# A mixture-of-experts kernel: expert choice in short pieces, scaled identities on ScalarE, late tiles summed on TensorE

## The reference, cut to what matters

```python
q = (xb @ w_q).reshape(PEER_BLOCK, PEER_HEADS, 2, PEER_DHALF)
s = jnp.einsum('nhpd,hpkd->nhpk', q, keys)            # 128 keys in each half
top_s, top_i = lax.top_k(s, 16)
cand = top_s[:, :, 0, :, None] + top_s[:, :, 1, None, :]
cand_idx = top_i[:, :, 0, :, None] * 128 + top_i[:, :, 1, None, :]
best_s, best_j = lax.top_k(cand.reshape(..., 256), 16)
idx = jnp.take_along_axis(cand_idx, best_j, axis=-1)
gsm = jax.nn.softmax(best_s, axis=-1)
act = jax.nn.gelu(jnp.einsum('nd,nhkd->nhk', xb, expert_u[idx]))
out = jnp.einsum('nhk,nhkd->nd', gsm * act, expert_v[idx])
```

## Time and profile before

| | before |
|---|---|
| median of three runs | 2196.28 us |
| the profiled execution | 2195.12 us |
| its span | 2193.3 us, granted PE clock 0.904 |
| busy: PE, DVE, POOL, ACT | 1674.3, 1528.5, 702.3, 466.5 us |
| fetches of expert rows | 576, 604.02 MB, 70.2% of the 16 DMA engines' span |
| weights and the rest | 123.92 MB, 17.4% |

### The profile page before, as it was taken

The page is one execution under the profiler, slowest core; times in us unless marked ns, Lnnn a source line. Parts: engine busy times, 40 slices in busy tenths (PEclk is TensorE's granted clock), DMA queues, the critical chain, the costliest instruction groups (busy, mean ns, idle before and its releaser), DMA issues.

```text
span 2193.3 us, 16524 instructions
## 1 busy us (share of the span) xinstructions
PE 1674.3 (76%) x5012; PEld 877.3 (40%) x5012; DVE 1528.5 (70%) x3429; ACT 466.5 (21%) x1250; POOL 702.3 (32%) x581
## 2 busy tenths in 40 slices
PE   8999977799978999979596556566655667666665
PEld 3699964344434455545252222222222222222221
DVE  2351248999977656658857888868787767767666
ACT  1061023222266420132211111112011111111111
POOL 0000013233322333223333343343433444445442
PEclk9999988999989999989798887788788899998898
DMA  8766578899878899969888998999898999999996
GB/s 276 251 200 218 195 246 319 329 340 352 309 275 290 313 363 378 351 245 377 330 323 331 356 348 344 359 369 381 327 354 336 374 412 403 420 413 413 404 408 282
DMA packets 203475, 730.08 MB, mean 333 GB/s; under 512 B 12957, under 2 KB 125991, under 8 KB 129521
## 3 DMA queue, kind: packets, MB, share of 16 engines
q0 software_dynamic: 82944, 604.02, 70.2%
q1 hardware_dynamic: 119190, 123.92, 17.4%
q10 hardware_dynamic: 1252, 1.09, 0.2%
HBM read 725.92 MB, written 3.06 MB: 332 GB/s over the span
## 4 chain that ended last, share of the span: by engine, by line
PE 37%; DMA 24%; DVE 23%; issue 10%; ACT 3%; POOL 2%; DVEq 0%; SPq 0%; ACTq 0%; POOLq 0%
DMA t_uv_rows<-in_expert_uv,t_arena 22%; PE bank L563 19%; PE v_sum L645 13%; PE bank L519 4%; DVE t_acc L1253 3%; DVE t_uv_rows L1237 3%; DMA t_uv_rows<-in_expert_uv,t_idx 2%; POOL t_uv_rows L484 2%; DVE t_diag L1261 1%; DVE t_arena L1210 1%; DVE t_arena L1211 1%; DVE t_arena L1212 1%; DVE t_arena L1155 1%; DVE t_arena L1156 1%; DVE t_arena L1159 1%
## 5 line engine op out<-in xcount | busy, mean ns | idle before, releaser
L645 PE MATMUL v_sum<-t_uv_rows,t_diag 128*128 128x512 f32 (+1 forms) x1536 | 855.1, 696 | 468.6 <-DVE t_diag L1261 468.4
L645 PEld LDWEIGHTS v_sum<-t_uv_rows,t_diag 128*128 128x128 f32 (+1 forms) x1536 | 307.0, 214 | 962.7 <-DVE t_diag L1261 661.7
L484 POOL DMA_INDIRECT t_uv_rows<-in_expert_uv,t_arena x384 | 464.5, 1210 | 634.2 <-PE v_sum L645 516.5
L1237 DVE CUSTOM_DVE_ANT_0 t_uv_rows<-t_uv_rows,t_arena 128x1024 f32<-128x1024 f32 x384 | 470.1, 1224 | 263.6 <-DMA t_uv_rows<-in_expert_uv,t_arena 259.1
L563 PE MATMUL bank<-t_arena,t_weights 128*128 128x192 f32 (+1 forms) x2560 | 642.2, 410 | 1.3 <-issue 0.9
L563 PEld LDWEIGHTS bank<-t_arena,t_weights 128*128 128x128 f32 x2560 | 453.4, 192 | 196.7 <-issue 47.3
L484 POOL DMA_INDIRECT t_uv_rows<-in_expert_uv,t_idx x192 | 237.4, 1236 | 831.9 <-PE v_sum L645 417.9
L821 ACT ACTIVATE t_gelus<-t_dots 128x1 f32<-128x1 f32 x576 | 115.4, 202 | 1402.8 <-DVE t_dots L1237 1402.6
L1237 DVE CUSTOM_DVE_ANT_0 t_uv_rows<-t_uv_rows,t_tok 128x1024 f32<-128x1024 f32 x192 | 234.9, 1224 | 99.7 <-DMA t_uv_rows<-in_expert_uv,t_idx 97.1
L1253 DVE SCALAR_TENSOR_TENSOR t_acc<-t_uv_rows,t_wts,t_acc 128x1024 f32<-128x1024 f32 x187 | 239.6, 1281 | 1.7 <-ACT t_wts L826 1.7
L1261 DVE TENSOR_SCALAR t_diag<-t_ident,t_gelus,t_arena 128x128 f32<-128x128 f32 x288 | 99.0, 344 | 3.6 <-ACT t_gelus L821 3.6
(11 more groups left out here) (162 smaller groups left out, 966.5 us busy)
## 6 DMA issues: line engine op xcount, KB each, us to landing
t_weights<-in_w_in SPq DMA_DIRECT2D x40, 1024.0 KB, 5.9
t_weights<-in_w_ada SPq DMA_DIRECT2D x24, 1024.0 KB, 5.6
t_weights<-in_w_q SPq DMA_DIRECT2D x16, 1024.0 KB, 5.6
t_weights<-in_w_branch_a SPq DMA_DIRECT2D x8, 1024.0 KB, 7.0
t_weights<-in_w_branch_b SPq DMA_DIRECT2D x8, 1024.0 KB, 5.3
t_weights<-in_w_out SPq DMA_DIRECT2D x8, 1024.0 KB, 6.8
t_uv_rows<-in_expert_uv,t_arena POOLq DMA_INDIRECT x384, 8.6
t_weights<-in_keys_t SPq DMA_DIRECT2D x20, 256.0 KB, 7.3
```

Of the source, the lines that this page charges most:

```text
L484: pool.indirect_dma_start(out=uv_rows[:, slot % NUV, :], out_offset=None, in_=A["expert_uv"], in_offset=bass.IndirectOffsetOnAxis(ap=idx_o ...
L645: ins = nc.tensor.matmul(v_sum[0:m, half], scaled, v_row(slot)[:, half], start=opens, stop=False)
L1237: V.tensor_tensor_reduce(out=row, in0=row, in1=h2_rows(t), scale=1.0, scalar=0.0, op0=ALU.mult, op1=ALU.add, accum_out=dots[:, k:k + 1]).t ...
```

## The change

The three parts of a choice unit become eleven: one for each of four key halves ("keytop", "key"), the sums ("sums"), one "best" for each of two heads, "parts", "match", "number" and "gates". Within key and best, instructions of different heads no longer run as a batch; each is linked to the one before. The pieces are dealt over more places: units of tiles 0 and 1 over places 1 to 31, those from (2, 2) to (4, 3) over the 160 places from `dense + 5` (before: over 51 places and then 40 places from `dense + 64`). The second eight queries of group 1 come one in each place from `dense`.

`on_vector` now takes slots 2, 5, 8, ... of tile 0 (21 of 64), four of five in tile 1 (102 of 128), and none in tiles 2 to 4. The scaled identity is built by ACT, behind the weight, with a scale column; it has six buffers. PE sums the two rows of a pair at the next place's beginning, ahead of that place's products, which is where the "sum" entry had them, but for one slot later. In tiles 2 to 4 the last row closes the sum, without a fold.

```diff
-NW, NUV, NDIAG, NBANK = 3, 6, 4, 6
+NW, NUV, NDIAG, NBANK = 3, 6, 6, 6
...
-    return [("keytop", t, y), ("pairtop", t, y), ("number", t, y)]
+    return ([("keytop", t, y)] + [("key", t, 4 * y + h) for h in (1, 2, 3)] + [("sums", t, y), ("best", t, 2 * y), ("best", t, 2 * y + 1)]
+            + [(k, t, y) for k in ("parts", "match", "number", "gates")])
...
+    start += [[u] for u in queries[:5] + first[:4] + [queries[5]] + first[4:7] + [queries[6]] + first[7:] + [queries[7]]]
...
+    deal(queries[8:] + [("tok", 1, 0), square, norm, ("ada", 0, 22), ("ada", 0, 23)], places, 0, PAIRS)
+    deal(choice_units(0, 1), places, 1, 5)
+    later = [u for t, y in ((0, 2), (0, 3), (1, 0), (1, 1), (1, 2), (1, 3)) for u in choice_units(t, y)]
+    deal(later, places, 5, CHOICE_PLACES)
...
+    deal(choice_units(2, 1), places, DENSE_PLACES + 1, dense + 4)
...
+        places[dense + n].append(unit)
+    deal([u for t, y in [(2, 2), (2, 3)] + [(t, y) for t in (3, 4) for y in range(4)] for u in choice_units(t, y)], places,
+         dense + 5, dense + 165)
...
+    first, dense = (TOPK * sum(TILE_STEPS[t] for t in tiles) for tiles in ((0,), group_tiles(0)))
+    return slot % 3 == 2 if slot < first else slot < dense and slot % 5 != 0
...
+            def sum_row(t, slot):
+
+                if on_vector(slot):
+                    return
...
+                opens = slot == min(n for n in tile_slots(t) if not on_vector(n))
+                closes = t > 1 and slot == tile_slots(t)[-1]
+                if opens and t:
+                    pe.wait_ge(v_read, t)
+                pe.wait_ge(diag_done, NTH_ROW[slot])
+                scaled = diag[:, (NTH_ROW[slot] - 1) % NDIAG, 0:m]
+                for half in (slice(0, 512), slice(512, D)):
+                    ins = nc.tensor.matmul(v_sum[0:m, half], scaled, v_row(slot)[:, half], start=opens, stop=closes)
+                ins.then_inc(v_tile if closes else pe_rows, 1)
+                if closes:
+                    pe.wait_ge(v_tile, t + 1)
+                    pe.sem_inc(pe_rows, 1)
...
+                for slot in tile_slots(t)[-2:]:
+                    sum_row(t, slot)
+                if t > 1:
+                    return
...
+                elif role == "pair":
+                    here = slot_of(g, b[0], 2 * b[1])
+                    for slot in (here - 2, here - 1):
+                        if slot in tile_slots(g):
+                            sum_row(g, slot)
...
+                    nc.scalar.activation(gelus[:, k:k + 1], dots[:, k:k + 1], ACT.Gelu_apprx_tanh).then_inc(gelu_done, 1)
+                    act.wait_ge(gelu_done, slot + 1)
+                    nc.scalar.activation(wts[:, k:k + 1], gelus[:, k:k + 1], ACT.Copy,
+                                         scale=gsm_of(t)[:, at:at + 1]).then_inc(weight_done, 1)
+                    if not on_vector(slot):
+                        nth_row = NTH_ROW[slot]
+                        if nth_row > NDIAG:
+                            act.wait_ge(pe_rows, nth_row - NDIAG)
+                        act.wait_ge(weight_done, slot + 1)
+                        m = NS if t == 0 else P
+                        unit = ident2[:, :] if t == 0 else ident[:, :]
+                        nc.scalar.activation(diag[:, (nth_row - 1) % NDIAG, 0:m], unit, ACT.Copy,
+                                             scale=wts[:, k:k + 1]).then_inc(diag_done, 1)
...
+            def key_top(t, h):
...
+                link(V.max(top_v[:, 0:8], s))
+                link(V.max_index(top_i[:, 0:8], top_v[:, 0:8], s))
+                link(V.match_replace(less, top_v[:, 0:8], s, LOWEST))
+                if j == 3:
+                    dve.sem_inc(taken["score"], 1)
+                link(V.max(top_v[:, 8:16], less))
+                link(V.max_index(top_i[:, 8:16], top_v[:, 8:16], less))
...
+            def pair_top(t, h):
...
+                link(V.max(v[:, 0:8], c))
+                link(V.max_index(j[:, 0:8], v[:, 0:8], c))
+                link(V.match_replace(less, v[:, 0:8], c, LOWEST))
+                link(V.max(v[:, 8:16], less))
+                link(V.max_index(j[:, 8:16], v[:, 8:16], less))
...
+            def value(t, slot):
+                if not on_vector(slot):
+                    return
...
-                    if nth_row > NDIAG:
-                        dve.wait_ge(pe_rows, nth_row - NDIAG)
-                    m = NS if t == 0 else P
-                    unit = ident2[:, :] if t == 0 else ident[:, :]
-                    at = i * TOPK + k
-                    V.tensor_scalar(diag[:, (nth_row - 1) % NDIAG, 0:m], unit, gelus[:, k:k + 1], gsm_of(t)[:, at:at + 1],
-                                    ALU.mult, ALU.mult).then_inc(diag_done, 1)
...
-                before, own = values_at(t, i, j)
+                here = slot_of(t, i, 2 * j)
                 dot(t, i, 2 * j)
-                for step, k in before:
-                    value(t, step, k)
+                if here > tile_slots(t)[0]:
+                    value(t, here - 1)
                 dot(t, i, 2 * j + 1)
-                for step, k in own:
-                    value(t, step, k)
+                value(t, here)
+                if here + 1 == tile_slots(t)[-1]:
+                    value(t, here + 1)
```

More of the change, by code:

```diff
@@ L166, in schedule @@
     queries = query_units(0)
-    (key, pair, number), (key1, pair1, number1), (key2, pair2, number2) = (choice_units(0, y) for y in range(3))
+    first = choice_units(0, 0)
     square, norm, *copied = first_units(1)
-    start += [[u] for u in queries[:5] + [key, queries[5], pair] + queries[6:8] + [number]]
+    start += [[u] for u in queries[:5] + first[:4] + [queries[5]] + first[4:7] + [queries[6]] + first[7:] + [queries[7]]]
     s = staggered(start, lambda n, after: [])
@@ L194, in pair_entries @@
         if after:
-            close = j == PAIRS - 1 and i == TILE_STEPS[t] - 1
-            return [("sum", "pair", t, (i, j))] + [("both", "final", t, 0)] * close
+            return [("both", "final", t, 0)] * (j == PAIRS - 1 and i == TILE_STEPS[t] - 1)
         return [("pair", "pair", t, (i, j))] + [("both", "final", t - 1, j + 1)] * (t > 0 and i == 0 and j < 3)
@@ L629, in rows_of @@
                 return NS if t == 0 else P
[L631 to L633 removed]
+            def sum_row(t, slot):
+                if on_vector(slot):
+                    return
                 m = rows_of(t)
[L635 to L644, removed]
[L645 to L646 removed]
+                opens = slot == min(n for n in tile_slots(t) if not on_vector(n))
[10 more added lines that the diff above has]
+                    pe.sem_inc(pe_rows, 1)
             def close_sum(t):
+                for slot in tile_slots(t)[-2:]:
+                    sum_row(t, slot)
+                if t > 1:
+                    return
                 m = rows_of(t)
[L651 removed]
+                pe.wait_ge(dve_rows, max(NTH_ROW[slot] for slot in tile_slots(t) if on_vector(slot)))
                 fold = ident2[:, :] if t == 0 else ident[:, :]
@@ L1118, in _ @@
             H2 = 2
+            DOUBLED = ((0, slice(0, NS)), (1, slice(NS, P)))
             def scratch(t):
@@ L1233, in dot @@
+                    batch(V.tensor_copy(gsm0[rows, 0, step], exps[rows, odd * TOPK:(odd + 1) * TOPK]) for odd, rows in DOUBLED)
             def dot(t, i, k):
@@ new lines, in value @@
+                if not any(on_vector(n) for n in range(tile_slots(t)[0], slot)):
+                    if t:
+                        dve.wait_ge(v_tile, t)
+                    V.tensor_scalar(acc[:, :], row, wts[:, k:k + 1], None, ALU.mult).then_inc(dve_rows, 1)
+                else:
+                    dve.wait_ge(dve_rows, nth_row - 1)
+                    V.scalar_tensor_tensor(out=acc[:, :], in0=row, scalar=wts[:, k:k + 1], in1=acc[:, :], op0=ALU.mult,
+                                           op1=ALU.add).then_inc(dve_rows, 1)
```

157 lines of the change are left out of this document (63 added, 94 removed).

## The result

The changed kernel takes 2091.55 us (median of 4 runs, 2081.8 to 2093.88) where the one before takes 2197.73 (4 runs): a ratio of 0.951, with a 95% interval from 0.9492 to 0.9527. The profiled execution took 2093.47 us, its span 2091.7.

The account below looks back on a forecast made before the run. PE bounds 724 to 945 us, DVE's order 1160 to 1745, DMA the rest from 1745. Terms +2.4 + 0 - 10 + 0 - 80 = -88 from 2195.12 us; forecast 2108 us, range 2060 to 2172.

Parts of the forecast that it names:

- the middle regime: 1160 to 1745 us: nothing full, 195 fetches in 585 us; forecast 503 us, -80 taken, ends -47 and -93.
- DVE sets the order: 1160 to 1745 us: DVE's 471 us of work plus 102 us waiting for rows make 573 of 585 us.
- DVE ceases to be the bound: From 1160 us on: DVE's load comes to 1.80 us per row, below the 2.548 us of a fetch.
- The identity's price: Scaled identity on ScalarE taken at 0.39 us, between 0.295 and 0.481; with weight and gelu 0.89 of 2.548 us per row.
- The 20 us that the rule would have cost: Row's way 0.34 us longer, were it the limit: 0.06 us per row, 20 us over 361 rows; not summed.
- Tiles 2 to 4 by PE alone: DVE loses 0.25 x 1.281 us of accumulation per row; PE gets a quarter more rows, 1.98 us each, covered.
- The choice in pieces: Eleven pieces: 20 new waits at 0.12 us, 2.4 us per unit, ends 0 and 5.6; first fetch +2.4 us.
- Tiles 0 and 1: Rows dealt anew: tile 0 taken at 0 (ends -10 and +22), tile 1 at -10 us (ends -67 and +10).
- more won: Rival: PE runs ahead in tile 1 (-35), tile 0 gives 5, tiles 2 to 4 -103: 2055 us; chance 0.14.
- DMA nearly bound: Rival: DMA share is already 0.92 from 1160 to 1745 us, so -47 instead of -80: 2141 us; chance 0.15.
- the ring's way: Rival: row's way 13.9 us of 15.3; 16.3 with a choice piece always before it: 2170 us; chance 0.10.
- Half clock: Rival: PE at half clock in row sums of tiles 2 to 4, 3.40 us per row: 2407 us; chance 0.06.

Follow-up runs that it names:

- the pieces by stage: Changed kernel with the choice cut by stage into ten pieces and every second of the 32 rows from slot 192 on DVE: 2074.19 us.
- the wait added: Changed kernel with ScalarE building a slot's identity only when the next slot's dot is done: 2117.58 us.
- the load alone: Changed kernel with DVE also multiplying a scaled identity into a tile nobody reads, behind the next dot: 2104.49 us.
- the best one: Changed kernel with choice cut by stage, every second of 32 rows from slot 192 on DVE, second eight queries in every third place: 2063.51 us.

## Why the prediction was right, and where its reasons were not

*The bound and the total.* 2108 us were forecast, 2091.55 came. DMA fills, as the middle regime was to become like the last: -84.6 us in the sixth stretch against -80. Fetches 2.57 us apart, clock 0.99 and DVE waiting for landings are the signs that were named.

*DVE sets the order: half right.* The step "DVE ceases to be the bound", by 1.80 us of load per row, leads to the right end by the wrong road. By its own sum the identity could have stayed on DVE (1.80 + 0.34 = 2.14 us, below 2.548) and the total would have been the same; so far the hit was luck. The kernel with the identity on DVE has 1.96 us of load per row and is slower at 2.62; with the same load and no wait, a row takes 2.57. What the change removed is a place in an in-order queue: an identity that stood behind another row's dot. The clause that says so stands in the prediction and was priced at nothing; as an edit of its own it measured some 26 us of the 47. The rows alone, which take 0.25 x 1.281 us of DVE's load per row, less what the added identities cost, and won next to nothing in these tiles (976.0 against 980.7 us), show the same from the other side.

*The identity's price.* 0.39 us were taken, 0.402 measured; ScalarE is covered, at 195 of 500 us. The wait for a free identity buffer cost 0.4 us in all (the last figure of line 837 above), so its price of nothing was right. The rule of the Trainium skill, "ScalarE: Activation LUTs", section "Rules for kernel authors", that a plain multiply belongs on VectorE, holds here for the single instruction (344 ns on DVE, 402 on ScalarE) and not for the kernel: moving it back costs 47 us. The figure that the Trainium skill gives beside that rule is for bf16, and this operation is fp32. The 20 us that the rule would have cost presume that the identity on DVE starts at once, and it did not.

*Tiles 2 to 4 by PE alone.* Counted as a gain of 0.32 us of DVE per row; worth nothing there, since DMA is full without it, as the kernel with the old rows shows. From slot 192 to 215 the forecast was 0, with ends of 8 either way; +6.0 came, and the same kernel (105.0 against 115.3 us to slot 224) puts the cause on PE, which was seen to be the bound there.

*The choice in pieces.* 2.4 us per unit for the added waits; 2.71 measured, and the first fetch comes 2.8 us later for +2.4. In tiles 0 and 1 the pieces cost 6.6 us, less than the 17 and 5 us of DVE's time that were charged; that the pieces by stage, with whole batches, do not pay it (734.6 us) speaks for the waits as its cause.

*Tiles 0 and 1.* -10 was forecast for them together, -22.4 came. The PE-bound stretch gave -12.1 for the 11 us that DMA's idle share was to allow, but not by that limit: DMA's share is 0.95 there as before, while its rate rose from 356 to 367 GB/s, and PE, at 191.56 of 208.9 us, is no longer full. The number came by luck; what holds that stretch now is open. The first stretch, tile 0 and four slots more, taken at nothing with -10 as its lower end, gave -10.6: PE could take the rows. A window of 40 us there, columns as above:

```profile
400.00:440.00 40.00, 40.00 (x121) 19.28 (x120) 38.17 (x94) 13.24 (x39) 13.12 (x12) 1.00 0.93 339
```

PE is full in it, but DVE is busy for 38.17 of the 40 us too, and the kernel that gave DVE more of tile 0's rows gained nothing; so PE is not shown to be the bound there.

The stretch from 566 us on, which the rival "more won" feared for, got 5.4 us longer, with ScalarE at 93 us instead of 86. The new dealing of rows wins 20 us in these tiles where the identity is on ScalarE (754.2 to 734.6 without the pieces, 762.7 to 741.2 with them) and nothing by itself (762.9 against 763.6). That nothing is a sum of two: tile 0 loses what tile 1 wins. Tiles 0 and 1 of the kernel before, then of the one with the rows alone:

```profile
310.60:560.70 250.10, 206.36 (x635) 102.97 (x636) 220.89 (x606) 60.57 (x166) 83.01 (x64) 0.91 0.91 343
560.70:1074.20 513.50, 451.24 (x1260) 242.69 (x1259) 368.85 (x671) 172.04 (x359) 154.32 (x128) 0.93 0.87 323
312.30:577.00 264.70, 223.88 (x675) 108.33 (x676) 216.84 (x624) 59.45 (x158) 73.51 (x65) 0.92 0.88 328
577.00:1075.20 498.20, 394.94 (x1115) 217.62 (x1113) 394.37 (x648) 180.95 (x391) 160.24 (x129) 0.89 0.87 329
```

In tile 0 more rows wait for an identity from DVE (43 instead of 32), and it takes 14.6 us longer; with the identity on ScalarE and the long parts in both kernels, the same edit costs 2.6 us there. That fits the wait, but no run takes it apart in this tile.

*The rivals.* "DMA nearly bound" (2141) and "the ring's way" (2170) did not come true, but the second was near: its 13.9 us is what five buffers measured, and one wait of 1.7 us more makes it bite. Half clock did not come: 0.99 over tiles 2 to 4, and the kernel with the old rows, with a quarter fewer rows on PE there, ran at 0.87 from slot 224 on and lost nothing by it. "More won" (2055) had the right direction for tiles 0 and 1.

## What to carry over

When buffers in a ring come free through a chain of engines, follow the way of one row from issue to reuse and look for the instruction that stands in an in-order queue behind work of another row: its wait counts against the ring's slack, and an engine that is only two thirds busy can hold the ring up so. Move that instruction to an idle engine even where it takes longer there. Cut long blocks between the rows, but along their batches, and take work off an engine only in the stretches where it is the one that is full.

## What the runs showed of the hardware beyond that

In these kernels, once DMA is full, a shorter way no longer brings fetches nearer to each other; it shows as longer landings. The median landing is 8.3 to 8.6 us in the kernels with some DMA share to spare (five buffers, the wait added, the identity on DVE) and 10.1 to 10.2 in those without (the changed kernel, the one with the load alone and the best one), at the same 1 MB; the kernel with the old rows, full as well at 414 GB/s, lies between with 9.1. A 128x128 Copy with one scale column takes 402 ns on ScalarE, against 294 for one column.
